# Two transformer blocks on one core: norm sums as columns and spread by TensorE, an early root table, the context norm moved between stages

## The reference, cut to what matters

```python
def rms_norm(x, w):
    y = xf * lax.rsqrt(jnp.mean(xf * xf, axis=-1, keepdims=True) + EPS)
    return (y * w.astype(jnp.float32)).astype(x.dtype)
...
    for layer in range(DEPTH):                      # first block, DEPTH = 2
        h = rms_norm(x, norm_mix_pre[layer])
        m = mixer_block(h, ..., w_out[layer])
        x = x + rms_norm(m, norm_mix_post[layer])
        h = rms_norm(x, norm_ffn_pre[layer])
        f = swiglu(h, w_ffn_gate[layer], w_ffn_up[layer], w_ffn_down[layer])
        x = x + rms_norm(f, norm_ffn_post[layer])
...
        hx = rmsnorm(x, norm1_w[l]) * (1.0 + sc1) + sh1      # second block
        hc = rmsnorm(xc, norm1_w[l]) * (1.0 + sc1c) + sh1c
        mix_x, mix_c = token_mixers(hx, hc, ...)
        x = x + g1 * mix_x
        hx = rmsnorm(x, norm2_w[l]) * (1.0 + sc2) + sh2
        x = x + g2 * conv_ffn(hx, ffn_w_up[l], ffn_conv_w[l], ffn_conv_b[l], ffn_w_down[l])
```

## Time and profile before

| | |
|---|---|
| Median of 3 executions | 2992.26 us (2989.22 to 2993.55) |
| The profiled execution, its own time | 2995.09 us |
| Its span | 2993.3 us |
| Granted clock of PE, mean | 0.969 |
| Busy share of the span: PE, PEld | 94%, 78% |
| Busy share: DVE, ACT, POOL | 49%, 44%, 50% |

### The profile page before, as it was taken

How to read it: one execution, slowest core, us unless ns; L and a number is a source line. 1 busy time by engine, 2 the same in 40 slices (tenths; PEclk the granted TensorE clock), 3 DMA queues, 4 the chain that set the end, 5 groups by cost and what they waited for, 6 DMA issues and landing times.

```text
span 2993.3 us, 40566 instructions
## 1 busy us (share of the span) xinstructions
PE 2799.6 (94%) x16014; PEld 2323.2 (78%) x16014; DVE 1465.2 (49%) x2351; ACT 1307.5 (44%) x2026; POOL 1504.4 (50%) x628
## 2 busy tenths in 40 slices
PE   7999999989999979989999989899998999998999
PEld 6888688788878858756777767688887868888788
DVE  5576532457663247843443341432335845445655
ACT  5464444445454443353333323342433554434554
POOL 5568678456767844311223324344444424445687
PEclk9999999999999989989999999999998999999999
DMA  5358676335867523201111212223232313223455
GB/s 193 126 176 279 215 261 201 127 110 185 275 226 265 185 93 98 71 29 41 58 64 64 71 56 86 76 98 96 95 99 93 106 49 99 86 98 115 146 185 167
DMA packets 144866, 386.37 MB, mean 129 GB/s; under 512 B 11824, under 2 KB 64304, under 8 KB 144688
## 3 DMA queue, kind: packets, MB, share of 16 engines
q1 hardware_dynamic: 144688, 383.87, 38.7%
HBM read 382.77 MB, written 1.05 MB: 128 GB/s over the span
## 4 chain that ended last, share of the span: by engine, by line
issue 37%; POOL 29%; PE 28%; DVE 4%; ACT 1%; POOLq 0%; DMA 0%; DVEq 0%; ACTq 0%
POOL w_lo L929 29%; PE bank L986 8%; PE bank L990 4%; PE bank L970 3%; PE bank L972 3%; PE bank L971 3%; PE bank L1358 1%; PE bank L1328 1%; DVE sd L1786 1%; DVE bank L2194 1%; PE bank L1035 1%; PE bank L1295 1%; PE bank L1280 1%; PE bank L1073 1%; PE bank L1024 0%
## 5 line engine op out<-in xcount | busy, mean ns | idle before, releaser
L929 POOL TENSOR_TENSOR w_lo<-raw,w_hi 128x1024 fp32r<-128x1024 f32 x624 | 1504.2, 2421 | 1478.5 <-ACT w_hi L1390 1476.1
L1390 ACT ACTIVATE w_hi<-raw 128x1024 fp32r<-128x1024 f32 x624 | 655.1, 1053 | 428.3 <-PE bank L972 184.5
L970 PE MATMUL bank<-hl,w_hi 128*128 128x256 f32 (+1 forms) x2088 | 731.7, 350 | 59.3 <-DVE hl L2113 27.5
L971 PE MATMUL bank<-hl,w_hi 128*128 128x256 f32 (+1 forms) x2088 | 709.8, 340 | 0.0
L972 PE MATMUL bank<-hl,w_lo 128*128 128x256 f32 (+1 forms) x2088 | 709.6, 340 | 0.0
L970 PEld LDWEIGHTS bank<-hl,w_hi 128*128 128x128 f32 x2088 | 406.5, 195 | 125.2 <-issue 56.7
L971 PEld LDWEIGHTS bank<-hl,w_hi 128*128 128x128 f32 x2088 | 407.9, 195 | 43.7 <-issue 5.0
L972 PEld LDWEIGHTS bank<-hl,w_lo 128*128 128x128 f32 x2088 | 407.1, 195 | 40.8
L986 PE MATMUL bank<-hl,w_hi 128*128 128x512 f32 x1368 | 364.3, 397 | 14.2 <-DVE hl L2372 5.4
L986 PEld LDWEIGHTS bank<-hl,w_hi 128*128 128x128 f32 x1368 | 247.1, 190 | 63.4 <-issue 22.3
L990 PEld LDWEIGHTS bank<-hl,w_lo 128*128 128x128 f32 x1368 | 192.6, 191 | 19.5 <-DVE hl L1799 3.4
(11 more groups left out here) (290 smaller groups left out, 4232.3 us busy)
## 6 DMA issues: line engine op xcount, KB each, us to landing
raw<-stream SPq DMA_DIRECT2D x624, 512.0 KB, 3.4
spare_lo<-stream SPq DMA_DIRECT2D x32, 512.0 KB, 5.6
mix<-stream SPq DMA_DIRECT2D x32, 512.0 KB, 5.6
spare_hi<-stream SPq DMA_DIRECT2D x32, 512.0 KB, 5.6
xs<-x_rows SPq DMA_DIRECT2D x4, 256.0 KB, 4.3
xs<-ctx_rows SPq DMA_DIRECT2D x1, 1024.0 KB, 14.6
out_rows<-xs SPq DMA_DIRECT2D x8, 128.0 KB, 2.9
cst<-consts SPq DMA_DIRECT2D x1, 896.5 KB, 10.6
```

The costliest lines, as they stand in the source:

```text
L929: nc.gpsimd.tensor_tensor(w_lo[:, unit % SPLIT, :], raw[:, unit % RAW, :], w_hi[:, unit % SPLIT, :], ALU.subtract).then_inc(lo_ready, 1)
L970: nc.tensor.matmul(acc, wh, x[:, 0, k, c0:c1], start=k == 0, stop=False)
L971: nc.tensor.matmul(acc, wh, x[:, 1, k, c0:c1], start=False, stop=False)
L1390: nc.scalar.activation(w_hi[:, n % SPLIT, :], raw[:, n % RAW, :], ACT.Copy).then_inc(hi_ready, 1)
```

## The change

- **Sums as columns.** `token_sums` takes a row of squares as weights and a single column of ones as moving data, 128 tokens at a time, so the sums of 256 tokens stand as two columns of `STAT`. `token_roots` and `token_inverses` work on these 2 or 4 columns. `spread_inverse` brings the reciprocals back over all partitions: the column, broadcast to 128x128, is the weights, and the identity the moving data. The result `inv_root` lies in `X[4]`, which is bank 7, and the scaled rows read it there.
- **Bank 7 leaves `MANY`.**
- **Root table.** It is loaded ahead of the squares; at the query norms of the attention (`query_roots`) only for 0 and 3.
- **Squares added in PSUM.** `add_square` accumulates in `STAT` and writes `work` only with the last.
- **Context norm.** In the first block's last down product ACT squares the context, DVE adds, PE sums with one matmul behind the first tile, ACT takes the root, DVE the reciprocal and the rows (in `X[0]` to `X[3]`), two rows to each tile. Gains and halves are set there as well. At the head of the second block only latents are left.
- **Modulation units.** `PRE1` has 2 in place of 5, `GATES` 16 and 20 in place of 14 and 17, `FFNS` 16 in layer 0 in place of 15.
- **Constants.** The first piece brings the identity beside the ones.

```diff
-    counts = spread(14 if l < DEPTH - 1 else 17, GATES[4:])
-    for place, n in ((POST1, 2), (MID1, 4), (PRE1, 5)):
+    counts = spread(16 if l < DEPTH - 1 else 20, GATES[4:])
+    for place, n in ((POST1, 2), (MID1, 4), (PRE1, 2)):
         counts[place] += n
-    for place, n in enumerate(spread(15 if l < DEPTH - 1 else 20, FFNS[3:NFF - 3])):
+    for place, n in enumerate(spread(16 if l < DEPTH - 1 else 20, FFNS[3:NFF - 3])):
...
-FEW, MANY, WITH_STAT, THREE = [0, 1], [0, 1, 3, 4, 5, 6, 7], [0, 1, 2], [0, 1, 3]
+FEW, MANY, WITH_STAT, THREE = [0, 1], [0, 1, 3, 4, 5, 6], [0, 1, 2], [0, 1, 3]
...
+
+    inv_root = X[4]
+    root_col, inv_col = sd[:, T2 - 8:T2 - 4], sd[:, T2 - 4:T2]
+
+    def ctx_row(k):
+        return X[k % 4][:, 0:SEQ]
...
-                    sp.dma_start(ones, consts[:, 0:P]).then_inc(ones_loaded, 16)
+                    sp.dma_start(cst[:, 0:2 * P], consts[:, 0:2 * P]).then_inc(ones_loaded, 16)
...
+            def token_sums(row, c0, c1, first, last):
+
+                for j in range(c0 // P, c1 // P):
+                    done = nc.tensor.matmul(STAT[:, j:j + 1], row[:, j * P:(j + 1) * P], ones[:, 0:1],
+                                            start=first and j == c0 // P, stop=last, skip_group_check=True)
+                return done
+
+            def stat_free():
+                if at["stat"]:
+                    E.need(std_ready)
+                at["stat"] += 1
+
+            def spread_inverse(c0, c1):
+
+                E.need(inv_ready)
+                for j in range(c0 // P, c1 // P):
+                    last = nc.tensor.matmul(inv_root[:, j * P:(j + 1) * P], inv_col[:, j:j + 1].to_broadcast([P, P]), ident,
+                                            start=True, stop=True)
+                last.then_inc(inv_spread, 1)
+
             def last_rows_sum(c0, c1):
 
-                row_sum(0, 2, work[:, 0, c0:c1], c0, c1)
+                E.need(sq_ready)
+                stat_free()
+                token_sums(work[:, 0, :], c0, c1, True, False)
                 E.need(sq_tile, KD)
-                nc.tensor.matmul(STAT[:, c0:c1], ones, work[:, KD - 1, c0:c1], start=False, stop=True)\
-                    .then_inc(stat_ready, 1)
-
-            def norm_sum(k, c0, c1):
-                row_sum(k, KD, work[:, k, c0:c1], c0, c1)
+                token_sums(work[:, KD - 1, :], c0, c1, False, True).then_inc(stat_ready, 1)
+                spread_inverse(c0, c1)
 
             def norm_sums(c0, c1):
+                stat_free()
                 for k in range(KD):
-                    norm_sum(k, c0, c1)
+                    E.need(sq_ready)
+                    last = token_sums(work[:, k, :], c0, c1, k == 0, k == KD - 1)
+                last.then_inc(stat_ready, 1)
+                spread_inverse(c0, c1)
...
-                product_halves(hid, 0, SEQ, KD - 1, fresh=ff_ready)
+                product_halves(hid, 0, SEQ, 1, fresh=ff_ready)
+                if l == DEPTH - 1:
+                    pe.wait_ge(ctx_square_sum, 1)
+                    nc.tensor.matmul(STAT[:, 0:SEQ], ones, work[:, 0, 0:SEQ], start=True, stop=True).then_inc(ctx_sum, 1)
+                product_halves(hid, 0, SEQ, KD - 2)
                 product(hid, 0, SEQ)
+                if l == DEPTH - 1:
+                    pe.wait_ge(ctx_root, 1)
                 modulation_at(l, POST2)
...
-                    norm_sums(0, T2)
+                    norm_sums(SEQ, T2)
+                    pe.wait_ge(ctx_ready, KD)
...
+            def token_roots(c0, c1):
+
+                E.need(stat_ready)
+                cols = slice(c0 // P, c1 // P)
+                nc.scalar.activation(root_col[:, cols], STAT[:, cols], ACT.Sqrt, bias=eps[:, 0:1], scale=1.0 / D)\
                     .then_inc(std_ready, 1)
...
                 c0, c1 = LAT
+                nc.scalar.preload_act_table(ACT.Sqrt)
+                if with_ctx:
+                    act.wait_ge(ctx_loaded, 16)
+                    act.wait_ge(ff_rows, NFF * DEPTH)
+                    for k in range(KD):
+                        square(k, xs, 0, SEQ, ctx_squares)
                 for f in range(KD - 1):
                     n = next_tile()
                     E.later(tile_done, 1)
                     act.wait_ge(tile_out, n + 1)
                     square(f, mix, c0, c1, sq_tile)
+                    if with_ctx and f == 0:
+                        act.wait_ge(ctx_sum, 1)
+                        nc.scalar.activation(sd[:, 0:SEQ], STAT[:, 0:SEQ], ACT.Sqrt, bias=eps[:, 0:1], scale=1.0 / D)\
+                            .then_inc(ctx_root, 1)
+                    if with_ctx and 1 <= f <= KD // 2:
+                        act.wait_ge(mod_ready, MODS * DEPTH)
+                        for k in (2 * f - 2, 2 * f - 1):
+                            act.wait_ge(ctx_rows, k + 1)
+                            nc.scalar.activation(h_hi[:, k, 0:SEQ], ctx_row(k), ACT.Identity,
+                                                 bias=mod[:, 0, k, 0:1]).then_inc(ctx_hi, 1)
...
+            nc.scalar.preload_act_table(ACT.Sqrt)
             E.need(eps_ready)
             c0, c1 = LAT
             for l in range(DEPTH):
                 squares_of_x(c0, c1, updated=l > 0)
-                root(c0, c1, D)
+                token_roots(c0, c1)
...
-                        root(c0 if i < AG else 0, T2, AD, query_roots(i))
+                        root(c0 if i < AG else 0, T2, AD, query_roots(i), i in (0, 3))
...
+            def token_inverses(c0, c1):
+                E.need(std_ready)
+                cols = slice(c0 // P, c1 // P)
+                V.reciprocal(inv_col[:, cols], root_col[:, cols]).then_inc(inv_ready, 1)
+                E.need(inv_spread)
...
-                    last = V.tensor_tensor(work[:, 0, c0:c1], work[:, 0, c0:c1], work[:, k, c0:c1], ADD)
+                    total = work[:, 0, c0:c1] if k == 1 else STAT[:, c0:c1]
+                    dst = STAT[:, c0:c1] if k < KD - 2 else work[:, 0, c0:c1]
+                    last = V.tensor_tensor(dst, total, work[:, k, c0:c1], ADD)
...
+            def add_ctx_squares():
+                for k in range(KD):
+                    dve.wait_ge(ctx_squares, k + 1)
+                    if k:
+                        total = work[:, 0, 0:SEQ] if k == 1 else ctx_row(0)
+                        last = V.tensor_tensor(ctx_row(0) if k < KD - 1 else work[:, 0, 0:SEQ], total, work[:, k, 0:SEQ], ADD)
+                        if k < KD - 1:
+                            C.do(last)
+                            C.settle()
+                last.then_inc(ctx_square_sum, 1)
+
+            def ctx_norm(f):
+                if f == 1:
+                    dve.wait_ge(mod_ready, MODS * DEPTH)
+                    set_gains(0)
+                    set_halves()
+                    dve.wait_ge(ctx_root, 1)
+                    C.do(V.reciprocal(X[4][:, 0:SEQ], sd[:, 0:SEQ]))
+                    C.settle()
+                for k in (2 * f - 4, 2 * f - 3):
+                    if 0 <= k < KD:
+                        dve.wait_ge(ctx_hi, k + 1)
+                        V.scalar_tensor_tensor(h_lo[:, k, 0:SEQ], ctx_row(k), mod[:, 0, k, 0:1], h_hi[:, k, 0:SEQ],
+                                               ADD, SUB).then_inc(ctx_ready, 1)
+                for k in (2 * f - 2, 2 * f - 1):
+                    if 0 <= k < KD:
+                        if k >= 4:
+                            dve.wait_ge(ctx_ready, k - 3)
+                        V.scalar_tensor_tensor(ctx_row(k), xs[:, k, 0:SEQ], gain[:, 0, k, 0:1], X[4][:, 0:SEQ],
+                                               MUL, MUL).then_inc(ctx_rows, 1)
...
                 for k in range(KD + 1):
                     if k < KD:
                         written.append(C.do(V.scalar_tensor_tensor(work[:, k, c0:c1], mix[:, k, c0:c1], v_(name, l, k),
-                                                                   sd[:, c0:c1], MUL, MUL)))
+                                                                   inv_root[:, c0:c1], MUL, MUL)))
```

78 lines of the change are left out of this document (46 added, 32 removed).

## The result

The changed kernel takes 3059.68 us (median of 4 executions, 3057.67 to 3064.36), against 2992.91 us before (4 executions): 66.8 us more, a ratio of 1.0226 with a 95% interval of 1.0208 to 1.0244. It is slower. The profiled execution has a span of 3059.0 us against 2993.3.

A forecast was written before the change was run, and what follows sets the result against it. The prediction took PE, busy 94% of the span, to bound the kernel. From the profiled 2995.1 us, less 28 (norms), plus 70 (bank waits) and 35 (clock), it got 3072, against a forecast median of 3069 us; range 3032 to 3092.

The forecast's parts named there:

- The bank wait: Second block's feed-forward of layer 0: with six banks PE waits 3.88 us for DVE's low part, 18 times, 70 us.
- The clock: Behind those 18 waits PE falls to 1.2 GHz, losing 1.95 us each, 35 us (0 to 55).
- The norms: All norm parts together: 14.4 in holes, 0.9 at the start, 16 between blocks, less 3: 28 us gained (22 to 35).
- The moved context norm: Between the blocks: first tile ends 17.3 us sooner, less 1.3 us of new waiting; net 16 us gained (13 to 20).
- The addition in PSUM: Behind the first block's output products: DVE's late additions no longer run late, root starts 1.3 us sooner in both layers.
- No gain, no loss: Token sums in the norms: 0.46 us a row against 0.69 now, paced by the squares, so nothing gained or lost.
- the 1.0 us for each of the norms with eight rows: Norms with 256 tokens: root to scaled row falls from 2.30 to 1.3 us, gaining 1.0 each.
- the rival in which the holes don't shrink: In the holes PE's clock is at half, passes take twice as long, 28 shrinks to about 10: 3087 us; chance 0.12.
- The query roots' table loads: Attention's query norms: loads dropped there free ACT only, since DVE ends last; gain nothing.
- The modulation units: Six units leave the holes, where they cost nothing, for gates and feed-forward, where PE is full: 3 us lost.
- That the bank wait doesn't come: Rival, same feed-forward: low part done before PE asks, so only the norms count: 2964 us; chance 0.05.
- That the clock mostly holds: Rival, same feed-forward: fewer than half of the waits lower the clock, 15 us lost: 3049 us; chance 0.18.

The follow-up runs named there:

- e1: The change with bank 7 back in MANY (seven banks), nothing else: 2961.71 us, ratio 0.9893 to the kernel before.
- e2: The kernel before with six banks in MANY (bank 7 out), its norms untouched: 3089.95 us, ratio 1.0326.
- e5: The change with its six banks, ACT's high and DVE's low part of pair t-2 ahead of pair t's convolution in the second block's feed-forward: 2974.43 us.
- e3: The change with 14 unread matmuls of 512 columns put into 16 of the 18 bank waits: 3040.68 us, ratio 1.0166.
- e6: The change with seven banks and the context norm back at the head of the second block: 2980.23 us, ratio 0.9945.
- e11: The change with seven banks and the squares added in SBUF as before: 2966.31 us, ratio 0.9916.
- e9: The change with seven banks; norms with eight successive rows of squares back to wide sums without spread, table still loaded early: 2961.6 us, ratio 0.989.
- e10: The change with seven banks and the root's table loaded at every query norm again: 2965.75 us, ratio 0.9907.
- e8: The change with seven banks and the modulation units back at their old places: 2964.74 us, ratio 0.9899.

## Why the prediction was right, and where not

The time was inside the range, and 66.8 us came where 77 were forecast. The main mechanism was right; several of its smaller terms were not, and some of their errors cancelled. Step by step:

- **The bank wait** was right in place, number and cause: 18 waits, each ended by DVE's low part (e1, e2, e5). The forecast said that PE would start 3.88 us later; it starts 1919.31 - 1915.29 - 0.225 = 3.79 us later than it could. The rows call it 3.63, since the record of the last matmul reaches beyond its step. PE's timeline at three resumed tiles, behind the first of which the clock stayed full:

```profile
1985.50 0.50 PE L981 MATMUL bank<-hl,w_hi 128*128 128x512 f32 x1 [3.63 <-DVE hid L2528]
...
2000.35 0.50 PE L981 MATMUL bank<-hl,w_hi 128*128 128x512 f32 x1 [3.63 <-DVE hid L2528]
...
2016.77 0.50 PE L981 MATMUL bank<-hl,w_hi 128*128 128x512 f32 x1 [3.63 <-DVE hid L2528]
```

  From the first to the second it is 14.85 us, against 48 x 0.225 = 10.8 for a pair without a wait. That is 4.0 for a wait with its slower first steps, 72 us in all against the forecast's 70.
- **The clock** is the term that was mis-sized. Forecast 35 us; 95.6 - 72 = 24 measured, and 20.5 of them came back in e3. The mechanism held. But the mean of 3.9 us for each wait came from eight mixed waits in other places. Here intervals with a slow stretch are mostly 16.4 us long (2000.35 to 2016.77), 1.6 more than without, and four of the eighteen waits, as that before 1985.50, have none of their own. The mean over all 18 is 24 / 18 = 1.3 us lost for each wait, against the 1.95 of the forecast. The Trainium skill (TensorE: Matmul & The Clock Gate, "HAM oscillation — how this bites in real kernels") counts 1.67 us at the low clock behind each of its DMA waits of 3 to 5 us, half of which is lost; by it all 18 waits would lose an estimated 15 us, as the prediction said. These traces agree on the fall and not on its size: an interval with a slow stretch loses 1.6 us, about twice that.
- **The norms** came to 29.9 us where 28 were forecast, but the parts don't match, and 1.9 us of it are the wait of the next item. The moved context norm was right in sum (17.4 us with the first tile against 17.3; e6), by two misses that cancel: the first product was put 1.8 us behind the sums and starts 3.7 behind them (1085.94 to 1089.66), and the first tile was put at 9.5 us and takes 7.2. The addition in PSUM was right (e11). "No gain, no loss" for the token sums failed, and with it the 1.0 us for each of the norms with eight rows. A row's sums were costed at 0.46 us; they take 0.58 to 0.61 at full clock and up to 1.01 at half. So they end 1.7 us behind the last square (336.19 to 337.90), where the wide ones ended 0.8 behind it (338.81 to 339.65). From last square to first scaled row the norm ahead of layer 0's feed-forward takes 3.59 us (336.19 to 339.78) against 3.67 before, where the row starts at 342.48:

```profile
342.48 1.28 DVE L1795 SCALAR_TENSOR_TENSOR work<-xs,vec,sd 128x256 f32<-128x256 f32 x3
```

  This is the mechanism of the rival in which the holes don't shrink, at work in these norms only: the norm behind the output product begins at full clock, and gained 2.5 us where 2.3 were forecast. The second block's layer 1 gained 2.9 against 1.6, but that is in part chance: with the norms of before the same stretch is 13.27 us in the kernel before and 11.90 in e2, and with the new ones 10.37 in the changed kernel and 12.00 in e9, where its sums take 3.57 us instead of 1.95. So the 12.9 us of the holes against 14.4 are made up of errors of opposite sign, and that they came so near is luck.
- **The query roots' table loads**, costed at nothing because DVE ends last there, were worth a wait of 1.94 us (e10). The step missed that ACT's time sets POOL's, and POOL's a DVE operation's.
- **The modulation units** were costed at 3 us; the stretches grew by 2.0 with all else, and e8 shows that the holes had no room for them any more. The step took it that in the holes the units cost nothing, which was so only while the norms were longer; as a cost of the change the term is nothing.
- **The other rivals.** That the bank wait doesn't come fell with the first timeline. That the clock mostly holds fell too: its condition was that fewer than half of the waits bring it down, and 14 of 18 did. Its 15 us lie about as far below the 24 measured as the forecast's 35 lie above.

No version here is faster than e1 by more than the medians can tell. The change with one number put back, 2961.7 us, beats both kernels: 1.1% less than before.

## What to carry to other kernels

When a buffer is taken out of a rotation, follow one round of it through the engine that frees it: the wait is the distance from the last use to the free, and it comes back at every tile if it depends on the tile just before. Look whether the two uses of the buffer meet in time at all before giving it to one of them. A wait of 3.6 us in dense matmuls cost its length and, in the mean, 1.3 us more for the clock here. Narrow matmuls on 128x128 weights gained nothing where the clock was at half behind them.
